# Latent attention by pairs of heads: rope halves stacked, one value product for two heads, softmax scaling on ScalarE, VectorE in another order

## The chip, the core and the metric

One core of a Trainium2 chip. The time is device microseconds from the start to the end of one execution; the kernel before takes 1957.33 us, the median of 3 runs (1956.78 to 1957.35).

## The reference, cut to what matters

Four transformer layers follow one another over 256 context and 256 latent tokens of width 1024: latent attention (layer 0), gated linear attention, a short convolution, and an mLSTM; each has a four times wider squared-relu MLP. Shift, scale and gate rows of every layer come from a vector by a large matrix product. The change is in the mixer of layer 0, with 8 heads:

```python
cq = rms_norm(h_all @ w_dq, g_q)                     # 512 x 384
q = (cq @ w_uq).reshape(B, T, 8, 128 + 64)           # 128 columns without rope, 64 with it
ckv = h_all @ w_dkv
kv = (rms_norm(ckv[..., :256], g_kv) @ w_ukv).reshape(B, T, 8, 128 + 128)   # keys, values
q_rope, k_rope = ...                                 # rotated for the 256 latent tokens only
s = einsum(q_nope, k_nope) + einsum(q_rope, k_rope)  # k_rope is one for all heads
p = softmax(s * 192 ** -0.5);  o = einsum(p, v)
y = o.reshape(T, 1024) @ w_o
```

Latent queries see all 512 tokens, context queries the 256 context tokens.

## The kernel before, in words

**Numbers.** A float32 weight block is split into a high and a low part (type fp32r); `mm3` (L721 to L732) makes one product of three single-pass matmuls: high by high (L725), high by low (L731), low by high (L732). `mm` (L734) on plain float32 operands is one instruction that shows as two records in the trace.

**The weight ring.** SP loads the blocks into 4 raw buffers. `take` (L391) is called by every engine once for each block, in its own program: it first splits the block four ahead, so that ring buffer n mod 5 is filled again (`split`: ScalarE writes the high part, L1608 to L1613, after waiting until the block five before was used; VectorE the low one, L2249 to L2257, after ScalarE), and then calls `pump`, which adds `rate` to a credit and performs one background unit for each whole credit. A unit on VectorE is four operations of 512 columns that add to the modulation sums of two token types (L2262 to L2287; the first of a sum has two plain multiplications, L2278). Its operands come by POOL's DMA into three buffers. A `close` of kind finish follows some units later: TensorE transposes the sum into a PSUM bank (L787), VectorE reduces it (L2348). For the gate rows (parts 2 and 5) it is ScalarE's high copy, VectorE's low part and a product with ones. Slots near the ends of a stage are `quiet`, and `ensure` does what is still missing when a stage needs it.

**PSUM.** Eight banks in one queue: `take` pops the front one, `give` puts it at the end at once, and TensorE waits before its first write until whoever read the bank eight takes ago has emptied it.

**The attention.** Blocks: per head one of 192 query columns by 384 rows (3 x 192 = 576 columns wide in the buffer) and one of 256 by 256 (512 wide). TensorE's order for h = 0 to 8 (L1147 to L1157): `queries(h+1)` (the 128 plain columns and the 64 rope columns, 9 matmuls of 512 columns each, L1053), `keys(h+1)` (keys 6 of 512, values 24 of 128 columns, rope rotation 64 x 64 by 256, L1071), `weights(h-1)` (12 transposes of the probabilities, L1109), `scores(h)` (L1093: plain and rope product for two latent tiles of 512 keys and two context tiles of 256), `values(h-1)` (L1121: twelve records of 256 columns into bank o). Below, pass h is what TensorE does from the end of `scores(h-1)` to the end of `scores(h)`. ScalarE copies queries and keys, takes exp with the row sum (L1872) and copies o (high part, L1886). VectorE copies the values (L2633) and the rope queries (L2625), rotates them (L2612 to L2616), finds the row maxima (L2643), negates and scales them (L2645), takes reciprocals (L2649), scales the probabilities (L2651), copies half of the transposed ones (L2660), and last in the pass subtracts for o's low part (L2665), which empties the bank of o. Its `take` calls stand at the head of `queries` and `keys`. `proj_last` then multiplies by w_o in 4 takes of 24 matmuls each, followed by `ensure` for the gate rows.

## Time and profile before

| | |
|---|---|
| median of 3 runs | 1957.33 us |
| profiled execution, its own time | 1955.74 us |
| its span, first to last instruction | 1953.9 us |
| mean granted TensorE clock | 0.998 |
| DMA | 315.16 MB, mean 161 GB/s |

Busy time is a union of an engine's instructions; durations are in ns or us as marked, starts in us from the start of the span. A matmul's duration includes its way through the array, so successive starts give its pace. The numbers of records include one weight load (PEld) for each matmul.

### The profile page before, as it was taken

What the parts mean: (1) busy time and instruction counts of PE and PEld (TensorE: products, weight loads), DVE (VectorE), ACT (ScalarE), POOL (GpSimd) and SP (SyncE); (2) the same over time, 40 slices, a digit from 0 to 9 for tenths busy, and PEclk for the clock granted to TensorE, in tenths of its full rate; (3) what the DMA queues carried; (4) which work ended last, traced back from release to release, by engine and by line L of the source; (5) the groups of instructions that cost most, each with busy time, mean ns of one, the idle gap of its engine ahead of it and who ended that gap; (6) DMA issues with size and microseconds to landing.
All of it is one profiled execution on the core that took longest, in us unless ns stands there. A gap on an engine that the chain in (4) does not pass through costs nothing.

```text
span 1953.9 us, 27442 instructions
## 1 busy us (share of the span) xinstructions
PE 1908.0 (98%) x10261; PEld 1601.7 (82%) x10261; DVE 1404.8 (72%) x2250; ACT 899.7 (46%) x1541; POOL 251.4 (13%) x334
## 2 busy tenths in 40 slices
PE   8999999999999999999999999999999999889998
PEld 3877788888888786889988888888888878878997
DVE  5889777888866665487997676667755567667765
ACT  3433355333343553575554224634233454656554
POOL 2101010111110110411101001001110021331000
PEclk9999999999999999999999999999999999999999
DMA  8434235665663451368875422645555245337763
GB/s 310 138 97 141 70 104 183 208 191 173 195 191 103 142 184 33 98 228 265 267 243 168 145 98 75 199 158 184 162 172 162 78 152 173 98 97 228 230 194 116
DMA packets 191891, 315.16 MB, mean 161 GB/s; under 512 B 14693, under 2 KB 114368, under 8 KB 191760
## 3 DMA queue, kind: packets, MB, share of 16 engines
q1 hardware_dynamic: 162512, 210.09, 33.4%
q0 software_dynamic: 29248, 103.33, 17.4%
q8 instruction: 82, 1.34, 0.3%
q14 instruction: 49, 0.40, 0.1%
HBM read 312.32 MB, written 1.05 MB: 160 GB/s over the span
## 4 chain that ended last, share of the span: by engine, by line
PE 81%; DVE 9%; issue 4%; ACT 3%; DMA 2%; POOL 1%; SPq 0%; DVEq 0%; POOLq 0%; ACTq 0%
PE bank L725 24%; PE bank L732 22%; PE bank L731 22%; PE bank L735 8%; DVE w L2256 3%; DVE acc L2281 2%; PE bank L730 2%; PE bank L728 2%; ACT junk L1645 1%; PE bank L787 1%; POOL st L3281 1%; PE bank L811 1%; DMA raw<-in_mlp_w 1%; DVE X L2400 1%; ACT w L1613 1%
## 5 line engine op out<-in xcount | busy, mean ns | idle before, releaser
L1613 ACT ACTIVATE w<-raw 128x1024 fp32r<-128x1024 f32 (+4 forms) x390 | 399.1, 1031 | 542.0 <-PE bank L732 469.3
L2256 DVE TENSOR_TENSOR w<-raw,w 128x1024 fp32r<-128x1024 f32 (+3 forms) x372 | 438.8, 1188 | 220.6 <-ACT w L1613 220.2
L725 PE MATMUL bank<-HH,w 128*128 128x256 f32 (+1 forms) x1552 | 505.7, 326 | 3.4 <-DVE HH L2383 2.0
L731 PE MATMUL bank<-HL,w 128*128 128x512 f32 (+1 forms) x1232 | 412.3, 335 | 0.0
L732 PE MATMUL bank<-HH,w 128*128 128x512 f32 (+1 forms) x1232 | 412.1, 335 | 0.0
L2281 DVE SCALAR_TENSOR_TENSOR acc<-ada,sc,acc 128x512 f32<-128x512 f32 x518 | 362.2, 745 | 2.3
L725 PEld LDWEIGHTS bank<-HH,w 128*128 128x128 f32 x1552 | 290.6, 187 | 30.4 <-issue 4.4
L725 PE MATMUL bank<-w,UH 128*128 128x512 f32 x768 | 300.7, 392 | 0.6 <-DVE UL L2558 0.6
L732 PE MATMUL bank<-w,UL 128*128 128x512 f32 x768 | 299.2, 390 | 0.0
L731 PE MATMUL bank<-w,UH 128*128 128x512 f32 x768 | 298.9, 389 | 0.0
L732 PEld LDWEIGHTS bank<-HH,w 128*128 128x128 f32 x1232 | 230.3, 187 | 26.0
L731 PEld LDWEIGHTS bank<-HL,w 128*128 128x128 f32 x1232 | 230.4, 187 | 25.6 <-issue 0.2
L732 PEld LDWEIGHTS bank<-w,UL 128*128 128x128 f32 x768 | 144.2, 188 | 30.3
L725 PEld LDWEIGHTS bank<-w,UH 128*128 128x128 f32 x768 | 144.2, 188 | 30.1 <-ACT w L1613 1.0
L731 PEld LDWEIGHTS bank<-w,UH 128*128 128x128 f32 x768 | 144.3, 188 | 29.1
L3218 POOL DMA_DIRECT2D ada<-in_mod_w x96 | 69.5, 725 | 525.1 <-DVE acc L2281 525.1
L725 PE MATMUL bank<-w,HH 128*128 128x512 f32 (+2 forms) x336 | 128.6, 383 | 1.9 <-issue 1.9
L732 PE MATMUL bank<-w,HL 128*128 128x512 f32 (+2 forms) x336 | 126.7, 377 | 0.0
L731 PE MATMUL bank<-w,HH 128*128 128x512 f32 (+2 forms) x336 | 126.5, 376 | 0.0
L2558 DVE TENSOR_TENSOR UL<-tp,UH 128x256 fp32r<-128x256 f32 (+1 forms) x128 | 69.7, 556 | 76.0 <-ACT UH L1804 75.6
L3218 POOL DMA_DIRECT2D ada<-in_ada_w x80 | 58.0, 726 | 353.4 <-DVE acc L2281 353.4
L1796 ACT ACTIVATE ta<-bank 128x256 f32<-128x256 f32 (+1 forms) x128 | 62.4, 488 | 79.1 <-PE bank L732 76.0
(365 smaller groups left out, 2605.2 us busy)
## 6 DMA issues: line engine op xcount, KB each, us to landing
raw<-in_mlp_w SPq DMA_DIRECT2D x256, 512.0 KB, 4.4
ada<-in_mod_w POOLq DMA_DIRECT2D x96, 512.0 KB, 4.7
ada<-in_ada_w POOLq DMA_DIRECT2D x80, 512.0 KB, 4.7
raw<-in_ml_w_qkvo SPq DMA_DIRECT2D x28, 512.0 KB, 3.8
raw<-in_conv_w_in SPq DMA_DIRECT2D x24, 512.0 KB, 4.1
raw<-in_ada_w SPq DMA_DIRECT2D x12, 512.0 KB, 6.2
raw<-in_mla_w_o SPq DMA_DIRECT2D x8, 512.0 KB, 4.0
raw<-in_gla_w_v SPq DMA_DIRECT2D x8, 512.0 KB, 3.8
```

The source lines that it names most:

```text
L725: pe.matmul(o, sh, mh, start=start, stop=False, skip_group_check=True)
L728: pe.matmul(o, sl, mh, start=False, stop=False, skip_group_check=True)
L730: return pe.matmul(o, sh, ml, start=False, stop=stop, skip_group_check=True)
L731: pe.matmul(o, sh, ml, start=False, stop=False, skip_group_check=True)
L732: return pe.matmul(o, sl, mh, start=False, stop=stop, skip_group_check=True)
L735: return pe.matmul(o, st, mv, start=start, stop=stop, skip_group_check=True)
L1613: act.activation(k.halves(n)[0], k.raw[(NDIRECT + n) % NRAW][:, 0:m], ACT.Copy).then_inc(*k.w_hi.up("w hi", n))
L1796: act.activation(t1[:, 0:N], b[:, 0:N], ACT.Relu).then_inc(*b.emptied())
L2256: dve.tensor_tensor(low, k.raw[(NDIRECT + n) % NRAW][:, 0:m], high.bitcast(F32), ALU.subtract).then_inc(*k.w_lo.up("w lo", n))
L2281: i = dve.scalar_tensor_tensor(out=o, in0=k.ada[m % NADA][:, q, :], scalar=cc, in1=o, op0=ALU.mult, op1=ALU.add)
L2558: dve.tensor_tensor(UL[:, n, 0:N], t2[:, 0:N], UH[:, n, 0:N].bitcast(F32), ALU.subtract).then_inc(*k.u_lo.up("u lo", li, q, n))
L3218: pool.dma_start(k.ada[m % NADA][:], src).then_inc(*k.ada_in[m % NADA].up("ada in", m, by=16))
```

## The change

- Heads go in pairs p. Weights: a block `first` of 3 x 256 columns (head 2p with its rope columns, and the rope columns of head 2p+1), `second` of 3 x 128, and `both` with keys and values of both heads (2 x 512). 12 blocks instead of 16; the stage has 28 slots instead of 32, and its rate goes from 1.2 to 1.6; slot 11 is quiet too.
- The 64 rope rows of the two heads are stacked into 128 rows: one query product, one rotation (the matrix is 128 x 128). For the scores the rope rows of a head are split: `QR` holds high and low part one above the other, `KRH` the high keys twice, `KRL` the low keys twice, and two fp32r matmuls take the place of the plain float32 one.
- One value product of 256 columns for two heads (24 matmuls a pair). It stands in the even passes, after `keys(h+1)`, and is the last reader of block `both`.
- The two context tiles of the scores share a bank, and so do those of the transposed probabilities: 3 banks instead of 4.
- ScalarE: multiplies the queries by 192 ** -0.5 as it copies them, copies the values, the rope queries and the high rope halves, the whole transposed context part, and scales the probabilities (`scaled`) behind its copy of o.
- VectorE: maxima negated as they are found, three instead of four, two reciprocals instead of four; subtracts for the low rope halves (`rope_low`). Its order: one `take` at the head of passes 1 to 6, then the low part of o of two heads before; a second `take` in odd passes, ahead of the maxima.
- In `whole` (L376 to L384) a chunk counts as whole where its step "leading" is still to be done; before, where "low" was. POOL's memsets of the rope rows go, its three constant loads are 128 rows high.

The core of the diff:

```diff
         a, e = self.at, self.at + LENGTH[li][which]
-        first, last = {(0, 0): (range(a + 5, a + 11), 4), (1, 0): (range(a + 1, a + 5), 16),
+        first, last = {(0, 0): (range(a + 5, a + 12), 4), (1, 0): (range(a + 1, a + 5), 16),
                        (3, 0): (range(a + 1, a + 9), 18)}.get((li, which), (range(a + 1, a + 5), 4))
         self.quiet = set(first) | set(range(e + 1 - last, e + 1))
...
     def whole(self):
 
-        whole = [end[1:4] for _, _, end in self.closing if end[0] == "low"]
+        whole = [end[1:4] for _, _, end in self.closing if end[0] == "leading"]
         closing, self.closing = self.closing, []
         for n, key, end in closing:
...
 
-    for name, h in [("q", 0), ("q", 1), ("kv", 0), ("kv", 1)] + [(name, h) for h in range(2, 8) for name in ("q", "kv")]:
-        c = 192 if name == "q" else 256
-        yield wide(A["mla_w_u" + name][0][:, h * c:(h + 1) * c].rearrange("(k p) n -> p k n", p=128))
+    WQ = A["mla_w_uq"][0].rearrange("(k p) n -> p k n", p=128)
+    WKV = A["mla_w_ukv"][0].rearrange("(k p) n -> p k n", p=128)
+    for p in range(4):
+        c = p * 384
+        first = (WQ[:, :, c:c + 192], WQ[:, :, c + 320:c + 384])
+        both = WKV[:, :, p * 512:(p + 1) * 512]
+        second = WQ[:, :, c + 192:c + 320]
+        for block in (first, both, second) if p else (first, second, both):
+            yield wide(block)
     yield from tokw(A["mla_w_o"][0], 0, D, 0, D)
...
+            self.KRH, self.KRL = sb("KRH", [128, 512], F32R, s1), sb("KRL", [128, 512], F32R, s1)
+            self.QR = [sb(f"QR{i}", [128, 512], F32R, s1) for i in range(2)]
-        self.VV = [self.Y[:, o:o + 512].rearrange("p (t n) -> p t n", t=4) for o in (2816, 3328, 0)]
+        self.VV = [self.Y[:, o:o + 1024].rearrange("p (t n) -> p t n", t=4) for o in (2816, 0)]
+        self.PTl = self.Y[:, 1024:2048].rearrange("p (k n) -> p k n", k=4)
+        self.PTc = self.Y[:, 2048:2560].rearrange("p (k n) -> p k n", k=2)
...
-LENGTH = [(32, 64), (33, 64), (32, 64), (37, 64)]
-RATE = [(1.2, 1.05), (0.65, 0.45), (0.4, 0.8), (0.8, 0.35)]
+LENGTH = [(28, 64), (33, 64), (32, 64), (37, 64)]
+RATE = [(1.6, 1.05), (0.65, 0.45), (0.4, 0.8), (0.8, 0.35)]
...
+        def rope_queries(p):
+            b = ps.take("rope", p)
+            w.wait_ge(*b.before())
+            w.wait_ge(*ps.of("qr", p).is_empty())
+            mm(b[:, 0:256], k.rot, k.qx[:, 256:512]).then_inc(*b.filled())
+            ps.give(b)
+
+        def from_queries(key, wh, wl, c):
+            b = ps.take(*key)
...
+            return b
+
+        def first_queries(p):
+
             n = walk.take()
             wh, wl = block_ready(n)
+            from_queries(("qr", p), wh, wl, 128)
+            block_used_with(n, from_queries(("qn", 2 * p), wh, wl, 0))
+
+        def second_queries(p):
+            n = walk.take()
+            wh, wl = block_ready(n)
+            block_used_with(n, from_queries(("qn", 2 * p + 1), wh, wl, 0))
+
+        both = {}
+
+        def keys(h):
+            if h % 2 == 0:
+                both[h // 2] = walk.take()
+            wh, wl = block_ready(both[h // 2])
+            c = h % 2 * 256
             b = ps.take("kn", h)
...
+        def pair_values(p):
+            n = both[p]
+            wv = [x.rearrange("p q (h n) -> p q h n", h=2)[:, :, :, 128:256] for x in block_ready(n)]
+            bs = [ps.take("v", p, j) for j in range(2)]
             for t in range(4):
+                b = bs[t // 2]
+                w.wait_ge(*b.before())
+                o = b[:, t % 2 * 256:t % 2 * 256 + 256].rearrange("p (h n) -> p h n", h=2)
                 for q in range(2):
-                    p = mm3(b[:, t * 128:t * 128 + 128],
-                            (k.CKH[:, q, t * 128:t * 128 + 128], k.CKL[:, q, t * 128:t * 128 + 128]),
-                            (wh[:, q, 128:256], wl[:, q, 128:256]), q == 0, q == 1)
-            p.then_inc(*b.filled())
-            block_used_with(n, b)
-            ps.give(b)
-            rope(h, k.qr[h % 2][0:64, :], ps.of("qr", h).is_empty())
+                    m = mm3(o, (k.CKH[:, q, t * 128:t * 128 + 128], k.CKL[:, q, t * 128:t * 128 + 128]),
+                            (wv[0][:, q], wv[1][:, q]), q == 0, q == 1)
+                if t % 2:
+                    m.then_inc(*b.filled())
+            block_used_with(n, bs[1])
+            ps.give(*bs)
 
...
+            def score(o, c, nk):
+                mm(o, k.qn[i][:, c:c + 128], k.kn[i][:, 0:nk], True, False)
+                mm(o, k.QR[i][:, c:c + 128], k.KRH[:, 0:nk], False, False)
+                return mm(o, k.QR[i][:, c:c + 128], k.KRL[:, 0:nk], False, True)
+
+            for t in range(2):
+                b = ps.take("s", h, 1, t)
+                w.wait_ge(*b.before())
+                score(b[:, :], 256 + t * 128, 512).then_inc(*b.filled())
+                ps.give(b)
+            b = ps.take("s", h, 0)
+            w.wait_ge(*b.before())
+            for t in range(2):
+                p = score(b[:, t * 256:t * 256 + 256], t * 128, 256)
+            p.then_inc(*b.filled())
+            ps.give(b)
...
-        queries(0)
+        first_queries(0)
         for f in (5, 3, 4):
             turned(f)
-        rope("k", k.krT[0:64, :], ps.of("cqT", 5).is_empty())
-        queries(1)
+        rope_keys()
+        second_queries(0)
+        rope_queries(0)
         keys(0)
         for h in range(9):
-            if 0 < h < 7:
-                queries(h + 1)
-            if h < 7:
+            if h % 2 and h < 7:
+                first_queries((h + 1) // 2)
                 keys(h + 1)
+                rope_queries((h + 1) // 2)
+            elif h % 2 == 0 and h < 8:
+                if h:
+                    second_queries(h // 2)
+                keys(h + 1)
+                pair_values(h // 2)
             if h > 0:
                 weights(h - 1)
...
+        def rope_queries(p):
+            b = ps.of("qr", p)
+            w.wait_ge(*b.full())
+            if p:
+                w.wait_ge(*at("rope lo", p - 1, 1))
+            act.activation(k.qx[:], b[:, :], ACT.Copy, scale=SC).then_inc(*b.emptied())
...
-                walk.take()
             b = ps.of("qn", h)
...
+        def rope_high(p, i):
+            r = i * 64
+            w.wait_ge(*at("roped", p))
+            if p:
+                w.wait_ge(*ps.of("s", 2 * p - 2 + i, 0).full())
+            act.activation(k.QR[i][r:r + 64, :], k.qx[r:r + 64, :], ACT.Copy).then_inc(*k.rope_hi.up("rope hi", p, i))
+
+        def pair_values(p):
+            for j in range(2):
+                b = ps.of("v", p, j)
+                w.wait_ge(*b.full())
+                if p >= 2:
+                    w.wait_ge(*ps.of("o", 2 * p - 3).full())
+                act.activation(k.VV[p % 2][:, 2 * j:2 * j + 2, :], b[:, :].rearrange("p (t n) -> p t n", t=2),
+                               ACT.Copy).then_inc(*b.emptied())
+
...
+        def scaled(h):
+            i = h % 2
+            rec = k.st_p[:, i, 2, :]
+            for half, P, j in ((1, k.Pl, 0), (0, k.Pc, 2)):
+                w.wait_ge(*at("p recip", h, half))
+                w.wait_ge(*ps.of("s", h, 0).is_empty())
                 for t in range(2):
-                    b = ps.of("s", h, half, t)
-                    st = k.st_p[:, i, half * 2 + t, :]
-                    w.wait_ge(*at("score max", h, half, t))
-                    if h >= 2:
...
+        rope_queries(0)
         queries(0)
         for f in (3, 4):
             turned(f)
         walk.take()
+        walk.take()
         queries(1)
+        keys_rope_high()
+        walk.take()
         keys(0)
+        rope_high(0, 0)
+        rope_high(0, 1)
         for h in range(9):
-            if 0 < h < 7:
+            if h % 2 and h < 7:
+                walk.take()
+                rope_queries((h + 1) // 2)
                 queries(h + 1)
-            if h < 7:
                 keys(h + 1)
+            elif h % 2 == 0 and h < 8:
+                if h:
+                    walk.take()
+                    queries(h + 1)
+                keys(h + 1)
+                pair_values(h // 2)
             if h > 0:
                 weights(h - 1)
+            if h % 2 and h < 7:
+                rope_high((h + 1) // 2, 0)
+                walk.take()
             if h < 8:
                 scores(h)
             if h > 0:
                 values(h - 1)
+            if h < 8:
+                scaled(h)
+            if h % 2 and h < 7:
+                rope_high((h + 1) // 2, 1)
...
+            w.wait_ge(*k.roped.last())
+            dve.tensor_tensor(k.ropet[0:n, :], b[0:n, 0:256], k.cs[0:n, 1, :], ALU.mult).then_inc(*b.emptied())
...
+        def rope_low(p, i):
+            r = i * 64
+            w.wait_ge(*at("rope hi", p, i))
+            dve.tensor_tensor(k.QR[i][64 - r:128 - r, :], k.qx[r:r + 64, :], k.QR[i][r:r + 64, :].bitcast(F32),
+                              ALU.subtract).then_inc(*k.rope_lo.up("rope lo", p, i))
...
+            b = ps.of("s", h, 0)
+            w.wait_ge(*b.full())
+            dve.reduce_max(mx[:, 2:4], b[:, :].rearrange("p (t n) -> p t n", t=2), AX.X,
+                           negate=True).then_inc(*k.score_max.up("score max", h, 0))
+
+        def reciprocals(h):
+            i = h % 2
+            tot, rec = k.st_p[:, i, 1, :], k.st_p[:, i, 2, :]
+            for t in range(2):
+                w.wait_ge(*ps.of("s", h, 1, t).is_empty())
+            dve.reciprocal(rec[:, 0:2], tot[:, 0:2]).then_inc(*k.p_recip.up("p recip", h, 1))
+            w.wait_ge(*ps.of("s", h, 0).is_empty())
+            dve.reciprocal(rec[:, 2:4], tot[:, 2:4]).then_inc(*k.p_recip.up("p recip", h, 0))
...
         for h in range(9):
+            if h % 2 == 0 and 0 < h < 8:
+                rope_low(h // 2, 1)
             if 0 < h < 7:
-                queries(h + 1)
-            if h < 7:
-                keys(h + 1)
+                walk.take()
+            if h > 1:
+                values(h - 2)
+            if h % 2 and h < 7:
+                rope((h + 1) // 2, k.qx, 128)
             if h > 0:
                 weights(h - 1)
+            if h % 2 and h < 7:
+                rope_low((h + 1) // 2, 0)
+                walk.take()
             if h < 8:
                 scores(h)
-            if h > 0:
-                values(h - 1)
+                reciprocals(h)
+        values(7)
```

## Rows read from the trace of the kernel before

**Rows 1.** The page: span, and busy us, share and instructions of each engine.
```profile
span 1953.9 us, 27442 instructions
...
PE 1908.0 (98%) x10261; PEld 1601.7 (82%) x10261; DVE 1404.8 (72%) x2250; ACT 899.7 (46%) x1541; POOL 251.4 (13%) x334
```

**Rows 2.** Stretch in the attention: us, busy PE, PEld, DVE, ACT, POOL, clock, DMA.
```profile
134.00:152.00 18.00, 18.00 (x94) 13.62 (x93) 16.82 (x38) 5.79 (x13) 2.17 (x3) 1.00 0.41 125
```

**Rows 3.** Timeline of TensorE (start, duration, instruction, count): scores 0, output 7.
```profile
98.25 0.59 PE L735 MATMUL bank<-krT,qr 128*128 128x256 f32 x2
...
227.54 1.03 PE L735 MATMUL bank<-PTc,Y 128*128 128x256 f32 x4
```

**Rows 4.** The same view: runs of single-pass matmuls of 128, 512 and 256 columns.
```profile
104.81 0.27 PE L732 MATMUL bank<-w,CKL 128*128 128x128 f32 x1
...
107.16 0.28 PE L732 MATMUL bank<-w,CKL 128*128 128x128 f32 x1
...
119.09 0.58 PE L725 MATMUL bank<-CQH,w 128*128 128x512 f32 x1
119.51 0.39 PE L731 MATMUL bank<-CQL,w 128*128 128x512 f32 x1
...
123.18 0.39 PE L732 MATMUL bank<-CQH,w 128*64 128x512 f32 x1
...
799.73 0.28 PE L731 MATMUL bank<-HL,w 128*128 128x256 f32 x1
...
801.58 0.28 PE L732 MATMUL bank<-HH,w 128*128 128x256 f32 x1
```

**Rows 5.** The same view: P^T V of one head, float32 products of 256 columns.
```profile
116.69 1.89 PE L735 MATMUL bank<-PTl,Y 128*128 128x256 f32 x8
118.41 1.03 PE L735 MATMUL bank<-PTc,Y 128*128 128x256 f32 x4
```

**Rows 6.** The same view: rope rotation, transposes, and a pass later the transposes again.
```profile
127.96 0.64 PE L735 MATMUL bank<-qr,Y 64*64 64x256 f32 x2
128.53 1.09 PE L1117 MATMUL bank<-ident,Pl 128*128 128x128 f32 x8
...
146.91 1.09 PE L1117 MATMUL bank<-ident,Pl 128*128 128x128 f32 x8
```

**Rows 7.** Groups of VectorE in the attention: count, busy us, mean ns, idle before.
```profile
L2643 DVE TENSOR_REDUCE st_p<-bank 128x1 f32<-128x512 f32 x16 | 10.9, 684 | 4.4 <-PE bank L735 4.4
...
L2651 DVE TENSOR_SCALAR Pl<-Pl,st_p 128x512 f32<-128x512 f32 x16 | 7.8, 487 | 0.6
...
L2256 DVE TENSOR_TENSOR w<-raw,w 128x1024 fp32r<-128x1024 f32 x4 | 4.9, 1216 | 0.7 <-ACT w L1613 0.7
```

**Rows 8.** Groups of ScalarE in the attention, same columns.
```profile
L1872 ACT ACTIVATE Pl<-bank,st_p 128x512 f32<-128x512 f32 x16 | 11.0, 687 | 35.9 <-DVE st_p L2645 35.8
...
L1886 ACT ACTIVATE HH<-bank 128x512 fp32r<-128x512 f32 x8 | 4.8, 598 | 12.9 <-PE bank L735 12.9
...
L1613 ACT ACTIVATE w<-raw 128x1024 fp32r<-128x1024 f32 x4 | 4.2, 1058 | 3.1 <-PE bank L732 3.1
```

**Rows 9.** Timeline of VectorE: a background step, the first operation of a finish, a sum's opening.
```profile
139.80 2.73 DVE L2281 SCALAR_TENSOR_TENSOR acc<-ada,sc,acc 128x512 f32<-128x512 f32 x4
142.46 0.68 DVE L2348 TENSOR_REDUCE sums<-bank 128x4 f32<-128x512 f32 x1
143.37 0.88 DVE L2278 TENSOR_SCALAR acc<-ada,sc 128x512 f32<-128x512 f32 x2
```

**Rows 10.** A stretch with the clock as its third number from the end; TensorE's rows there.
```profile
108.00:112.00 4.00, 4.00 (x16) 3.10 (x17) 3.90 (x9) 0.98 (x2) 0.72 (x1) 0.57 0.65 197
...
107.94 0.61 PE L735 MATMUL bank<-qr,Y 64*64 64x256 f32 x2 [0.51 <-DVE qr L2625]
108.49 1.94 PE L1117 MATMUL bank<-ident,Pl 128*128 128x128 f32 x8
```

**Rows 11.** Waits in the attention: total us, times, longest us.
```profile
PE bank L735 <- DVE sums L2348: 2.2, 1, 2.2
```

254 lines of the change are left out of this document (120 added, 134 removed).

## The prediction

> **What bounds the kernel now.** I read the page first, then the table of stretches, then TensorE's own rows. TensorE is busy for 98% of the span, VectorE for 72%, ScalarE for 46% [rows 1]. In the attention the table tells more: of a stretch of 18 us TensorE fills 18.00 at full clock, VectorE 16.82, ScalarE 5.79 [rows 2]. So TensorE bounds this part, VectorE stands close behind it, and ScalarE has room. The first head's scores end at 98.68 us (98.25 and two records of 0.215), the last head's P^T V at 228.40 (227.54 and four) [rows 3].
>
> **TensorE's part, step by step.** Starts of successive records give the pace: single-pass matmuls take (123.18-119.51)/16 = 0.229 us at 512 columns, (107.16-104.81)/21 = 0.112 at 128 and (801.58-799.73)/16 = 0.116 at 256 [rows 4]. Twice the columns cost almost nothing below 256. A plain float32 product is two records: at 256 columns they pace 0.215 (eight in 118.41-116.69), so 0.43 us, and twice that, 0.86, at 512 [rows 5].
> - Rope part of the queries: one matrix of 128 rows for two heads, so 9 of 36 products a pair go: 4 x 9 x 0.229 = 8.2 us.
> - Values: 48 products of 128 columns a pair become 24 of 256: 4 x (48 x 0.112 - 24 x 0.116) = 10.3 us.
> - Scores: the rope product becomes two single passes. Per head 2 x (0.86-0.46) + 2 x (0.43-0.23) = 1.2, by 8 = 9.7 us. No single pass follows a float32 product within one sum so far. The nearest switch: four P^T V records from 118.41 end their pace at 119.27, the next kind starts at 119.09, 0.18 early, and its follower comes 0.42 later, 0.19 late [rows 4, 5]. Both together are 0, the lateness alone is 0.2; I take 0, and up to 6.4 us for 32 switches as the bound.
> - Rope rotation: one instead of two a pair; from its start to the next 0.57 pass, 0.14 more than two records pace [rows 6]: 4 x 0.57 = 2.3 us. It may gain up to 0.6 more if the 128-row form has no such gap.
> Sum: 30.5, say 31 us less TensorE work. Alone it would give 1926. TensorE is the fullest engine by the page and by the stretch [rows 1, 2]. The Trainium skill, "Perfetto Trace Analysis", section Identifying Performance Opportunities, says that kernels generally improve by improving the most-contended engine; by this rule the sum would be 1926, a gain of 31, which is rival 1 below. No row of before contradicts it. What speaks against it here is the order of the waits, next.
>
> **VectorE and ScalarE.** VectorE loses, per head, the scaling of probabilities (0.49 and less for each of four), the negations, two reciprocals, the value copy, the query copy, half the rope and the context's P^T copy, and gains a 64-row subtraction; its four maxima become three of 0.68 [rows 7]. With 0.6 to 0.7 for an operation of 512 columns and two thirds of it for 256 that is some 4.5 us a head less. ScalarE gains four scalings, 2.0 us (nearest its 512-column copy 0.60), the value copy 0.6 and half-width copies [rows 8]; twice its 5.8 us a pass still leaves room. So no engine is over-full. The background modulation work doesn't shrink: a step costs 2.7 us (2.1 when it opens a sum), a finish 0.9 [rows 9], and at rate 1.6 it comes in lumps. Following the credit, VectorE's takes 12 to 20 hold: step-finish-step-finish; step; step, step, finish; step, finish; two steps; step, finish, step, finish; one; step, step, finish; step, finish.
>
> **The order is what I expect to decide.** Three facts of the diff meet. (a) The block with keys and values of both heads is last read by the pair's values, after the second query block is taken. A take splits the block four ahead into a ring of five, so in each even pass (heads 2, 4, 6) ScalarE's split waits until TensorE has finished the values. VectorE's low half waits for that, and its background steps stand behind. (b) VectorE now empties the output bank of head h-2 after the take, where it did so at the end of the pass. (c) Eight banks go round strictly: counting takes, the bank of o(h-2) is wanted again by a transposition of the same pass (the third in pass 2 and 6, the second in pass 4).
> Even pass 2, from the end T of head 1's scores: TensorE does P^T V 2.6 (12 records at 0.216 [rows 5]), a modulation column 0.36, queries 2.06, keys 1.38, values 2.8: T+9.2. ScalarE splits 768 columns 0.85: 10.1. VectorE: low 0.9, two steps 5.4, a finish 0.9, output 0.6: 17.9. TensorE resumes: last transposes 0.45, scores 3.95: T+22.3, where its own work is 14.5. Pass 4 has two modulation columns (9.6), 1024 columns to split (1.06 and 1.2: 11.8), two steps and two finishes (7.4), output 0.6, and two rows of transposes to go: T+24.7 against 14.8. Pass 6: 9.2, 1.06, 1.2, one step and finish 3.7, 0.6, 0.45, 3.95: T+20.2 against 14.5. Before, a pass is 18.38 (128.53 to 146.91) [rows 6].
> Odd passes: the last maximum ends at T+0.75, the exps of the context at 2.0 (two, somewhat under the 0.69 of 512 columns [rows 8]), the output copy 0.6 behind P^T V at 3.2, the scaling at 5.2; then ScalarE's split 1.06 and VectorE's low 1.2 end at 7.5 (6.5 in pass 1, which has no output). Pass 1: two steps and two finishes end at 13.7; the scores want the bank that the second finish empties at 13.5: 13.5 + 3.95 = 17.4. Pass 3: 7.5, step 2.7, finish 0.9, output 0.6 is 11.7; one transposition set 0.45 and scores 3.95: 16.1. Pass 5: opening step 2.1 and output 0.6 to 10.2, rope 1.1, P^T 0.6, rope low 0.6 to 12.5, split and low to 14.2, two steps and the sum of a finish to 20.3; the context scores (1.3) want that bank: 21.6. Pass 7 has no query work to hide the scaling: 5.2, two sets of transposes left, scores: 9.4. Tail: P^T V 2.6, scaling to 5.2, transposes and copies to 6.2, P^T V 2.6: 8.8.
> Sum from the first scores' end: 17.4 + 22.3 + 16.1 + 24.7 + 21.6 + 20.2 + 9.4 + 8.8 = 140.5, against 228.40-98.68 = 129.7: 10.8 more. Ahead of it queries 2.06, values 2.6, scores 1.2 and rope bubbles go: 7.2 less. The first rope chain (rotation 1.1, half-width copies 0.6 each on ScalarE, four subtractions 0.6 each and three splits on VectorE, all behind takes 9 and 10) ends at about 86.8 where TensorE asks at 98.68-7.2-3.95 = 87.5; it costs nothing, up to 3 if a load is late. Net +3.6.
> **Output projection.** Take 21 now holds two steps and the low halves, and take 22 the gate product that needs them: VectorE is done at 8.9 us after the attention, TensorE asks at 5.5 (24 x 0.229): about +3.
> **Clock.** A break of 0.51 us ahead of 107.94 was followed by a stretch at the lower of the two clock levels, 1.2 GHz: eight transposes took 1.94 instead of 1.09. Over 108 to 112 us the mean granted clock is 0.57, a loss of 4 x 0.43 = 1.7 us [rows 6, 10]. The longer break on the modulation sums, 2.2 us [rows 11], had no such fall. So a break costs 0 to 1.75. Mine last 6 to 10 us in four places: I take 1.75 for each, +7 (bounds 0 and 12).
> **Taken as nothing.** SP's loads (the first block of a pair comes in two pieces, 16 issues for 16 before), POOL's 128-row constants and the memsets that go: TensorE's work on the four blocks ahead hides them; a late one would show as a wait of the split for a DMA. The changed test for a whole chunk and slots moved by one in later layers: at most a wait like the 2.2 us [rows 11] here or there. Together -2 to +3.
> **Sum**: +3.6 + 3 + 7 = +13.6. The profiled execution, 1955.7 with 1953.9 of span, would become 1969.3; against the median of 1957.3 the forecast is 1971.
>
> **The rivals.**
> 1. *The order doesn't bind*: VectorE, relieved of 36 us, keeps ahead and TensorE runs dense: 1957.3 - 31 = 1926. For it: in the kernel before only 2.2 us of TensorE's time in the attention went to a bank that a finish held [rows 11]. Against: that row shows the very kind of wait, at 1.2 steps a take and with the output emptied early. Chance 0.17.
> 2. *It binds in part*: only the three even passes and one odd stall, half as long, without the clock: -31 + 18 = 1944. Chance 0.16. Ends between 1936 and 1955.
> 3. *Slower still*: every one of the breaks, the short ones too, costs clock (7 x 1.75 = 12 instead of 7), each float32 switch its 0.2 (6.4) and the gate products wait on both chunks (3 more): 1971 + 14 = 1985 and above. Chance 0.08.
> The diff does what it says; I give nothing to the opposite.
> The forecast is itself the slower side; it turns at the point where new waits, clock included, exceed 31 us, and it counts some 45.
>
> **How the numbers follow.** Forecast 0.59, its own range 1959 to 1984; rivals 0.17, 0.16, 0.08. A change under 0.2% (3.9 us) is about what this measurement can't tell from none. Slower: 0.59 less a thin low edge of 0.02, plus 0.08 = 0.65; same 0.05, from the edges of forecast and rival 2; faster 0.30. The range leaves out half of rival 1 and nearly all of rival 3: 1930 to 1984.
>
> **What would show it.** Right: TensorE idle of 5 to 10 us before the second or third transposition in passes 2, 4 and 6, released by VectorE's output subtraction; ScalarE's split waiting 2 us and more for the values' matmuls; passes alternating about 17 and 22 us; the lower clock after the breaks. Single steps: values 24 x 0.116 a pair, rope product 0.46 and 0.23, scores 3.95 a head. Wrong: passes of 14 us with TensorE at 18.00 of 18.00, or VectorE idle while TensorE works.

## The result, and the profile after

The changed kernel takes 1990.04 us (median of 4 runs, 1987.36 to 1990.86) against 1957.05 of the kernel before, measured beside it (1956.25 to 1957.35): ratio 1.0167, 95% interval 1.0154 to 1.0181. It is slower, as forecast, but by 33 us where 14 were forecast, and the time lies above the range. The profiled execution took 1989.45 us with a span of 1987.7; before, 1955.74 and 1953.9.

The page of the changed kernel, beside [rows 1]:

```profile
span 1987.7 us, 27077 instructions
...
PE 1895.1 (95%) x10121; PEld 1595.5 (80%) x10121; DVE 1375.6 (69%) x2132; ACT 927.2 (47%) x1590; POOL 249.8 (13%) x331
```

Only ScalarE is a little fuller than before (47% against 46%). TensorE's busy time fell by 12.9 us only, because part of what is left ran at half clock. Below, "clock loss" is TensorE's busy time times (1 - granted clock), added up in stretches of 1 us. From 60 to 300 us it is 1.7 us before and 16.1 now, and TensorE's idle time there is 4.8 and 47.9. Over the whole span the clock loss is 3.4 and 19.3, so the work without it fell by 28.8 us. Stretches of the attention, with the columns of [rows 2]:

```profile
120.00:140.00 20.00, 11.99 (x62) 9.49 (x61) 9.42 (x15) 7.12 (x13) 1.45 (x2) 0.75 0.26 79
160.00:180.00 20.00, 10.01 (x63) 8.93 (x62) 14.04 (x26) 8.98 (x20) 2.89 (x4) 0.86 0.40 122
220.00:240.00 20.00, 12.71 (x57) 9.11 (x56) 9.45 (x17) 9.68 (x21) 0.72 (x1) 0.83 0.17 52
```

Where TensorE filled 18.00 of 18.00 us before, it now fills 50 to 64% in these three stretches (73% over passes 1 to 8, 97% before), while VectorE fills 47 to 70% and ScalarE 36 to 48%: no engine is short of time, they wait for each other in turn. TensorE's waits from 60 to 300 us (total us, times, longest):

```profile
PE bank L1170 <- DVE HL L2786: 16.3, 4, 8.0
PE bank L1161 <- DVE HL L2786: 10.0, 1, 10.0
PE bank L751 <- DVE sums L2474: 9.7, 2, 6.7
PE bank L1058 <- DVE Y L2710: 3.6, 1, 3.6
PE bank L1161 <- ACT Pl L1977: 2.8, 2, 1.4
PE bank L751 <- DVE accl L2450: 2.6, 1, 2.6
```

Before, the only entry above 1.2 us there was the 2.2 us of [rows 11]. Two of the new names are those that the prediction gave: the low part of o (HL) in front of the transposes, and the modulation sums in front of the scores. The fourth, a scaling of cq ahead of the attention, it did not have.

TensorE's timeline, the last score record of heads 0, 1, 2 and 7, and the last P^T V:

```profile
97.14 0.28 PE L751 MATMUL bank<-KRL,QR 128*128 128x256 f32 x1
...
117.37 0.28 PE L751 MATMUL bank<-KRL,QR 128*128 128x256 f32 x1
...
142.33 0.28 PE L751 MATMUL bank<-KRL,QR 128*128 128x256 f32 x1
...
243.79 0.28 PE L751 MATMUL bank<-KRL,QR 128*128 128x256 f32 x1
...
250.58 2.83 PE L751 MATMUL bank<-Y 128*128 128x256 f32 x12 [0.78 <-ACT Y L1987]
```

Start plus duration is the end of a head's scores. The differences of the eight ends are the passes 1 to 7: 20.2, 25.0, 16.4, 27.9, 23.3, 24.2 and 9.7 us, and pass 8 has 9.2 to the end of P^T V (253.2: twelve records at a pace of 0.215).

Pass 2 shows how a break is made. VectorE, and TensorE below it:

```profile
128.02 0.96 DVE L2382 TENSOR_TENSOR w<-raw,w 128x768 fp32r<-128x768 f32 x1 [3.75 <-ACT w L1673]
128.90 5.38 DVE L2407 SCALAR_TENSOR_TENSOR acc<-ada,sc,acc 128x512 f32<-128x512 f32 x8
134.20 0.68 DVE L2474 TENSOR_REDUCE sums<-bank 128x4 f32<-128x512 f32 x1
134.92 0.16 DVE L2427 TENSOR_TENSOR mod<-sums,bgc 128x4 f32<-128x4 f32 x1
135.11 0.69 DVE L2786 TENSOR_TENSOR HL<-bank,HH 128x512 fp32r<-128x512 f32 x1
```

```profile
126.82 1.03 PE L1161 MATMUL bank<-ident,Pl 128*128 128x128 f32 x8
135.86 1.11 PE L1170 MATMUL bank<-ident,Pc 128*128 128x128 f32 x4 [8.01 <-DVE HL L2786]
136.77 1.91 PE L751 MATMUL bank<-kn,qn 128*128 128x512 f32 x2
```

VectorE idles 3.75 us for ScalarE's split, does its low half, two background units (eight operations, 5.4 us) and a finish, and only then the subtraction that frees o's bank. The two float32 records behind the break take 1.91 us instead of 1.02: the clock is at its lower level.

The loss by stretches, each the difference of the two traces at the same work: first scores 1.3 us earlier (97.4 against 98.7 [rows 3]); end of the attention 24.8 later (253.2 against 228.4); first transposes behind the output projection 29.5 later (297.9 against 268.3); the same until 666 us; then +30.6 at 871, +30.2 at 1068, +34.6 at 1239, and 33.8 at the end.

### The profile page after: what moved, and what is told of

Its sections match the earlier page's. It is cut to its first block, busy times and chain, and to the rows that moved or that the text cites. A ratio compares the mean times of both kernels' runs of the same rounds, so it can differ in the third digit from the quotient of the medians.

```text
span 1987.7 us, 27077 instructions
## 1 busy us (share of the span) xinstructions
PE 1895.1 (95%) x10121; PEld 1595.5 (80%) x10121; DVE 1375.6 (69%) x2132; ACT 927.2 (47%) x1590; POOL 249.8 (13%) x331
## 4 chain that ended last, share of the span: by engine, by line
PE 78%; DVE 11%; issue 5%; ACT 4%; POOL 1%; DMA 1%; SPq 0%; DVEq 0%; POOLq 0%; ACTq 0%
PE bank L741 23%; PE bank L748 21%; PE bank L747 21%; PE bank L751 8%; DVE acc L2407 3%; DVE w L2382 3%; PE bank L746 2%; PE bank L744 2%; ACT junk L1705 1%; ACT w L1673 1%; PE bank L803 1%; POOL st L3413 1%; PE bank L827 1%; DVE X L2526 1%; DMA raw<-in_ada_w 1%
## 5 line engine op out<-in xcount | busy, mean ns | idle before, releaser
L1673 ACT ACTIVATE w<-raw 128x1024 fp32r<-128x1024 f32 (+2 forms) x386 | 398.3, 1040 | 552.8 <-PE bank L748 466.7
```

Source lines behind the costliest of these rows:

```text
L1673: act.activation(k.halves(n)[0], k.raw[(NDIRECT + n) % NRAW][:, 0:m], ACT.Copy).then_inc(*k.w_hi.up("w hi", n))
```

## The experiments

All times are medians of at least four runs; the kernel before took 1955.6 to 1956.9 in the groups. A ratio's 95% interval is about 0.0015 to either side, 3 us, so smaller differences between two versions are read from their traces or not at all. "The slots' work" below is what a slot's take brings: a split and background units (one chunk's quarter each, 2.7 us of VectorE). Later edits are shown against the one before.

**1. The low part of o ahead of the take.**

```diff
+            if h > 1:
+                values(h - 2)
             if 0 < h < 7:
                 walk.take()
-            if h > 1:
-                values(h - 2)
```

> Edit: VectorE makes the low part of o of the head before ahead of the slot's take (split and background unit) instead of behind it; nothing else. Theory (banks are held by several late readers, the o bank only the last of them): the modulation bank, whose sums VectorE also closes late, binds next; 3 to 8 us less than the changed kernel, and breaks of the transposes of Pl and Pc still there, with the modulation sums named as releaser. Rival (the o bank's order alone makes the breaks): the breaks of 8.0, 10.0 and 5.9 us go and with them their clock, 25 to 34 us less, about the time of the kernel before.

Measured: 1984.67, 5.4 less, and not the 25 to 34 of the rival. It is the theory's size and its next wait: the low part is named for 1.3 us, and the sums take over.

```profile
PE bank L751 <- DVE sums L2474: 24.4, 6, 6.8
PE bank L1170 <- DVE sums L2474: 5.7, 2, 3.7
...
PE bank L1161 <- DVE HL L2786: 1.3, 1, 1.3
```

26 us of waits left one name and 20 came back under another. A name in the list of waits says who was last, not what the time would be without it.

**2. One unit a slot in slots 1 to 4.**

```diff
-        self.credit += self.rate
+        self.credit += 1.0 if self.at <= 4 else self.rate
```

> Edit: one background unit a slot in slots 1 to 4, as before the change (4 units instead of 6), 1.6 a slot behind them. Theory: VectorE scales cq in time again, the first scores end 5 to 6 us earlier, and the two units that move into the attention passes give 0 to 3 of it back: 3 to 6 us less than the changed kernel. Rival (the start ahead of the attention is hidden by the passes' own breaks, which wait for VectorE anyway): 0 to 1 us less.

Measured: 2000.40, 10.4 more: both expectations missed. The first half held: queries start at 74.3 instead of 78.3 and the first scores end 3.8 us earlier. The two units came back in the passes (end of the attention only 1.1 earlier), and the rest was lost far away: against the kernel before the later stages stand at +27.3, +33.2, +38.3, +38.7, +41.8, +41.4, +44.8, and the end at +45.9. Run 5 looks into that.

**3. Keys and values ahead of the second queries** (TensorE, and ScalarE's copies in that order).

```diff
-                if h:
-                    second_queries(h // 2)
                 keys(h + 1)
                 pair_values(h // 2)
+                if h:
+                    second_queries(h // 2)
```

> Edit: in even passes TensorE takes the keys of the next head and the pair's values ahead of the second queries, and ScalarE copies in that order, so that the block of keys and values is free before the slot's split asks for it. Theory: the splits of passes 2, 4 and 6 come 1.5 to 3.3 us earlier, VectorE's take is shorter by that, and the breaks behind it too: 3 to 6 us less than the changed kernel. Rival (the split waits, but VectorE is late for its own units): 0 to 1 us less.

Measured: 1983.47, 6.6 less: with all else as it is, fact (a) of the prediction costs that much, at the place where it was put.

**4. The three together.**

> The three edits of this group together. Theory: the gains add, since they are at different places, and breaks above 5 us lose their half-clock stretches as well: 15 to 22 us less than the changed kernel, so still slower than the kernel before by 11 to 18 us. Rival (one chain through VectorE, so the edits overlap): 6 to 12 us less. Rival (the o bank alone): 30 us or more less, faster than the kernel before.

Measured: 1976.68, 13.4 less, between the theory's 15 to 22 and the first rival's 6 to 12. The attention ended at 230.2, 23 us earlier, twice the sum of the three alone (6.1, 4.3 and 1.1 by their traces): each had uncovered the next wait, and together they take both. But behind the output projection, where it stood at +5.0 against the kernel before, it lost 17.4 more up to the end, as run 2 did (18.7).

**5. The fraction that is carried on.** The rate is added up in slots, and what is left of a unit at the end of the attention goes into all later layers.

```diff
         self.rate = RATE[li][which]
+        if (li, which) == (0, 1):
+            self.credit = 0.0
```

> Edit: the changed kernel, and the fraction of a background unit that 17 slots of 1.6 leave over (27.2, so 0.2) is set to nothing at the start of layer 0's second half, as 17 slots of 1.0 left it before; the slots of all later units are then those of the kernel before. Theory (the 4.3 us that the changed kernel loses between 840 and 1205 us come from those moved slots): 4 us less than the changed kernel (3 to 5), and its break of 2.1 us near 1068 us back at 0.6. Rival (they come from the cores' clock or from chance): within 1 us of it.

Measured: 1992.75, 2.7 more, which neither expectation had. My count was wrong: the kernel before has 32 slots with 22 that add 1.2, which leaves 0.4 and not 0. So this was no return to its order. Repeated with `self.credit = 0.39999999999999925`, the kernel before's own value:

> Edit: the changed kernel, with the fraction of a unit that is carried into layer 0's second half set to 0.4, which is what 22 slots of 1.2 leave in the kernel before (with 27.2 it is 0.2, and the run with nothing was based on a wrong count). Theory: the later layers then meet the kernel before's order, so the marks from 666 us on stay 29.5 us behind and the time is 4 us less than the changed kernel, 1985 to 1987. Rival (later losses come from the time of arrival, not from the order): within 1 us of the changed kernel or above it.

Measured: 1988.79, only 1.3 less; the ratio (1.0161, 1.0146 to 1.0176) does not tell it from the changed kernel. But the trace agrees with the theory up to 1600 us: this kernel stands 27.9 us behind at 296 us, and 27.9, 27.9, 27.6, 27.6, 27.6 at the next five stages, where the changed kernel goes from 29.5 to 34.6. Then it loses 3.6 up to 1793 and 1.0 more behind, in the last layer, so that the stages behind the output projection cost 4.3 in all, as in the changed kernel. Over all runs, what these stages cost against the kernel before, by the fraction they start with: 2.8 to 5.0 us at 0.2, 9.2 to 13.9 at nothing, 17.4 and 18.7 at 0.8. At 0.4 it is 4.3 to 5.7 with the changed test in `whole`, and 2.5 and less with the old one (runs 10 and 12). Slots that move by one there are not free, and the fraction is not the only thing that counts.

**6. The three edits with the fraction at nothing, and closing ahead of the unit.** The edit of the second:

```diff
-        self.unit(unit)
+        if self.at > 24:
+            self.unit(unit)
         for c in self.closing:
             c[0] -= 1
         self.flush(0)
+        if self.at <= 24:
+            self.unit(unit)
```

> The three edits of the first group together, and the fraction set to nothing as in the run beside it. The three together ended the attention 23 us earlier than the changed kernel but lost 16 us against the kernel before in the later layers, with a fraction of 0.8. Theory (the fraction is what costs there): 14 to 16 us less than with the three alone, 1961 to 1964. Rival (the units left over for the output projection cost, whatever the fraction): 3 us less at the most.

> As the run before it in this group, and up to slot 24 VectorE closes modulation sums (one reduction and one addition, 0.9 us) ahead of the unit that makes them due, not behind it (2.7 us), so that their bank comes free by that much earlier. Theory (with o's bank out of the way the modulation banks bind): the breaks named by the sums, 20.6 us in six, shrink by 2.7 us each where a unit stood in front: 6 to 12 us less than the run before it. Rival (VectorE is short of time in the passes, so what is closed earlier is paid by later maxima): 0 to 2 us less.

Measured: 1974.34 and 1969.08. The first rests on the same wrong count and fell (2.3 less than the three alone, not 14 to 16); its rival held. Its stages behind the output projection still cost 13.9 us instead of 17.4. The second gave 5.3 of the 6 to 12: the attention ends 6.5 us earlier, so the time for which a modulation bank is held did bind.

**7. Units placed by hand.** First with `STEPS` of one or two a slot in slots 12 to 20 and extra places only behind the copy of P^T (passes 2, 4, 6, 7 and 8) and at the head of passes 7 and 8; then with one at the head of each pass, where VectorE idles.

> As the run before it in this group, and the background units go to places by hand: one in each of slots 1 to 4, two or three in each of passes 1 to 6, each at a place of its own (behind the copy of the turned probabilities in passes 2, 4 and 6), and two in each of passes 7 and 8, which had none; so none is left for a lump ahead of the output projection's end. Theory (lumps of two units, 5.5 us of VectorE, make the breaks; its total of work fits under TensorE's): breaks in the passes under 6 us in all, no stretch at half clock, 10 to 18 us less than the run before it, and below the kernel before (under 1950). Rival (VectorE's total binds): within 4 us of the run before it.

> As the hand-placed run, with: one unit of VectorE's at the head of each pass right behind the low part of o, where VectorE idles 3 us for the split, and one behind it in passes 1 to 6 (two in pass 6); none between the copy of the turned probabilities and the maxima; the low part of the second rope half behind that copy; one unit between the two scalings of cq and ckv; and the fraction of a unit that is carried into the later layers as the kernel before has it (22 slots of 1.2: 0.4; the expectation of the run with the fraction at nothing said 17 slots of 1.0, which is wrong). Theory: passes 1 to 6 take 14 to 16 us each, so 10 to 14 us less up to the output projection than the hand-placed run, and the 5 us that it lost against the kernel before behind 633 us stay away as well: 1944 to 1952. Rival (VectorE and ScalarE hand over too often for a pass of 15 us): 1955 to 1962.

Measured: 1964.35, then 1936.89. The first fell short of its 10 to 18 (4.7, which the intervals hardly tell from none): even passes were down to 15.4 and 14.6, passes 3 and 5 stayed at 23.4 and 23.6, because in the even pass two units and two finishes stood ahead of the copy of P^T, for which TensorE's next product then waited 5.0 us. The second took passes 2 to 6 to 15.2, 14.2, 14.6, 14.2 and 14.6 us, and was faster than its own range. The edit of the second against the changed kernel, besides those above (`pump(n)` adds n to the credit; a slot takes its number from STEPS; the other engines call it at the same places of their order):

```diff
+STEPS = {1: 1, 2: 1, 3: 1, 4: 1, 12: 1, 14: 1, 15: 1, 17: 1, 18: 1, 20: 2, 21: 1, 22: 1, 23: 1, 24: 1}
+HEAD = {1: 1, 2: 1, 3: 1, 4: 1, 5: 1, 6: 1, 7: 1, 8: 1}
+MID = {7: 1, 8: 2}
+PRE = 1
...
         for f in range(3):
             turned(f)
+        walk.pump(PRE)
         mean_square(1, 256)
...
-            if h % 2 == 0 and 0 < h < 8:
-                rope_low(h // 2, 1)
             if h > 1:
                 values(h - 2)
+            walk.pump(HEAD.get(h, 0))
             if 0 < h < 7:
                 walk.take()
...
             if h > 0:
                 weights(h - 1)
+            if h % 2 == 0 and 0 < h < 8:
+                rope_low(h // 2, 1)
+            walk.pump(MID.get(h, 0))
```

**8. Light units.** Is it the work between two hand-overs, or the hand-overs themselves? This kernel leaves out the middle accumulations of slots 12 to 20 and keeps every order, bank and split.

```diff
+                elif 12 <= walk.at <= 20 and not (q == 1 and ty == types[-1]):
+                    continue
                 else:
                     w.wait_ge(*added[ty])
                     i = dve.scalar_tensor_tensor(
```

> Edit: the changed kernel, and the background units of slots 12 to 20 leave out those accumulations of the modulation sums that are neither first nor last of their unit (three of four of 0.69 us each in most units; these sums, and so the output, are left incomplete); order, banks and splits are kept. Theory (VectorE's background work, held in lumps between the reads of the banks, makes the breaks): breaks of the passes from 36 us to under 10, no stretch at half clock, 28 to 36 us less than the changed kernel, 1954 to 1962. Rival (the order of hands between ScalarE and VectorE around o and the splits makes them, whatever the work between): 8 us less at the most.

Measured: 1962.92, 27.1 less, a little outside the expected range; the rival's 8 fell. In the passes TensorE's idle time went from 41.5 us to 21.7 and its clock loss from 12.7 to 5.9, so the breaks fell by half and not to under 10:

```profile
PE bank L1170 <- DVE HL L2788: 8.1, 2, 4.2
PE bank L1161 <- DVE HL L2788: 6.0, 1, 6.0
PE bank L751 <- DVE sums L2476: 4.0, 2, 3.0
```

So 27 of the 33 us hang on the time that VectorE's units take where they stand, though VectorE is busy for only 119.6 of the 200 us from 60 to 260.

**9. Filled breaks.**

```diff
+                for _ in range({(1, 1): 50, (3, 0): 60, (5, 1): 36}.get((h, t), 0)):
+                    pe.transpose(b[:, 0:128], k.ident[:], k.ident[:])
```

> Edit: the changed kernel, and TensorE turns the identity 50, 60 and 36 times into the bank that it owns, ahead of the last transposes before the breaks of 8.0, 10.0 and 5.9 us, so that most of each break is filled with work that nobody reads. Theory (a break of that length costs 2.1 to 2.7 us more behind it, because the clock is at its lower level from then on for 7 to 10 us): breaks down to about 2 to 3 us, the half-clock stretches near 140, 185 and 236 us gone, 4 to 7 us less than the changed kernel. Rival (the clock falls whatever fills the break, or VectorE's chain hides it anyway): within 1 us of the changed kernel.

Measured: 1985.91, 4.1 less with 146 transposes more (1982.8 to 1988.3 against 1987.4 to 1990.9; the two intervals of the ratio overlap a little). The break of 8.0 us became 5.6 of unread work and 2.5 of break. TensorE's stretches (busy, then granted clock); the changed kernel first, the filled one second:

```profile
130.00:140.00 10.00, 4.14 (x9) 0.50 0.52 157
...
180.00:190.00 10.00, 10.00 (x37) 0.77 0.11 42
220.00:230.00 10.00, 4.09 (x19) 0.78 0.34 105
```

```profile
130.00:140.00 10.00, 7.45 (x37) 0.83 0.45 139
...
180.00:190.00 10.00, 10.00 (x42) 0.90 0.01 2
220.00:230.00 10.00, 8.02 (x49) 1.00 0.36 105
```

The clock stayed at full level behind the third break (2.4 us of pass 6 came back) and fell for a shorter time behind the other two (0.7 and 1.0 us). In this trace 1.3 us came back in pass 1 too, where nothing was filled: the clock varies by that much without any edit. The clock loss in passes 2, 4 and 6 together went from 8.4 to 4.3 us. So a part of each long break's price is the clock, and not the wait. The Trainium skill, "TensorE: Matmul & The Clock Gate", section Loop structure matters more than you think, says that the loop nest decides whether matmuls stay at the fast clock; by this run the trace agrees, with the 8.4 and 4.3 us above. Here unread work in the loop stood in for read work.

**10. The old test for whole sums, and fewer late units.**

```diff
-        whole = [end[1:4] for _, _, end in self.closing if end[0] == "leading"]
+        whole = [end[1:4] for _, _, end in self.closing if end[0] == "low"]
```

The second has `20: 1` in STEPS and `MID = {8: 2}`.

> As the second hand-placed run, and the test by which a gate's sum that is due at once goes through one float32 product is the kernel before's again (it asks for the low part still to be made, the changed kernel's for both parts). VectorE's order behind the attention is then that of the kernel before, instruction by instruction; with the changed test one gate of the last layer makes a low part, and TensorE waits 2.2 us for it. Theory: 3 to 4 us less than the second hand-placed run (1933 to 1934), the wait of 2.2 us near 1700 us gone. Rival (the wait moves elsewhere in that layer): within 1 us of it.

> As the run before it in this group, with one unit less in pass 6 and none between pass 7's copy of the turned probabilities and its maxima; both go to the output projection (layer 0 keeps the changed kernel's test, the later layers the old one). Theory (a unit ahead of the copy costs TensorE 2.5 us in pass 7, one ahead of the maxima 3.3 us in pass 8): passes 7 and 8 take 10.5 to 11.5 us instead of 13.3 and 12.3, 2 to 5 us less, 1929 to 1932. Rival (the projection's slots give them back at its gate): within 1 us of it or above.

Measured: 1934.58 and 1928.73. The wait of 2.2 us on a gate's low part in the last layer (in the second hand-placed run and in the one with 0.4) is gone, and 2.3 us with it, where 3 to 4 were expected. The second keeps the changed test in layer 0, where the old one would close a sum whole without waiting for a high part that ScalarE has already begun. Its passes 7 and 8 take 11.8 and 11.1 instead of 13.3 and 12.1, and it is 5.9 us faster than the run before. Two things changed at once, and of the 7.4 us between the two traces only 2.5 lie in these passes: 2.2 lie ahead of the first scores, 1.7 of that a clock loss that the run before had there, and 2.7 behind the output projection. Its ratio to the kernel before is 0.986 (95%: 0.9846 to 0.9875). The largest waits of TensorE from 60 to 300 us (two more, of 0.7 and 0.4, end the list):

```profile
PE bank L1173 <- ACT Pl L1992: 2.7, 2, 1.9
PE bank L763 <- DVE Y L2800: 2.6, 2, 2.3
```

VectorE in its pass 5, units one at a time and o's bank freed first:

```profile
150.63 0.69 DVE L2805 TENSOR_TENSOR HL<-bank,HH 128x512 fp32r<-128x512 f32 x1 [0.84 <-ACT HH L2007]
151.23 2.73 DVE L2425 SCALAR_TENSOR_TENSOR acc<-ada,sc,acc 128x512 f32<-128x512 f32 x4
...
156.01 2.74 DVE L2425 SCALAR_TENSOR_TENSOR acc<-ada,sc,acc 128x512 f32<-128x512 f32 x4
```

The later stages stand at -29.3, -29.3, -29.4, -29.5, -29.5, -29.5, -29.5 against the kernel before: nothing moves behind the attention any more. The Trainium skill, "Perfetto Trace Analysis", section Optimization Strategy, says that a repeated bubble on the engine that should be full can mean too little PSUM for the next tile. Here the eight banks are the same in the changed kernel and in this one: their readers' order and the lumps were at fault, not their number.

**11. The rate alone, in both kernels.**

In the kernel before:

```diff
-RATE = [(1.2, 1.05), (0.65, 0.45), (0.4, 0.8), (0.8, 0.35)]
+RATE = [(1.6, 1.05), (0.65, 0.45), (0.4, 0.8), (0.8, 0.35)]
```

> Edit: the kernel before (not the changed one), with 1.6 background units a slot instead of 1.2 in layer 0's first half, so 6 instead of 4 in slots 1 to 4 and lumps of two in the heads' slots. Theory (the lump ahead of the attention costs 5 us of start by itself; the kernel before has its breaks filled by 31 us more of TensorE's work and its o bank is freed by ScalarE at once, so lumps cost it little): 2 to 8 us more than the kernel before, 1959 to 1965. Rival (lumps are what makes the changed kernel slow, in any order of work): 20 us more or above, 1977 or more.

Measured: 1980.25, 24.7 more, ratio 1.0124 (1.0107 to 1.0141). The theory fell and the rival held: this one number costs the kernel before three quarters of what the change cost. It is not the rate's share of the 33 us, though. The first half of layer 0 has 28 units in all, and with 22 slots at 1.6 all of them stand ahead of the attention's end, against 25 in the kernel before and 24 in the changed kernel; so its passes have lumps and more work. (The theory had one premise wrong besides: in the kernel before too o's bank is emptied by VectorE, at the end of the pass.) Its trace shows the same row ahead of the attention, with the first scores 6.2 us later, and breaks in the passes with clock behind them (clock loss in the passes 8.3 us instead of 1.7):

```profile
PE bank L735 <- DVE qr L2625: 5.3, 2, 3.0
PE bank L735 <- DVE sums L2348: 4.4, 2, 3.3
PE bank L1042 <- DVE Y L2585: 3.6, 1, 3.6
```

Taking the rate back in the changed kernel is no cure, since it has 28 slots in that half instead of 32:

> Edit: the changed kernel, with 1.2 background units a slot instead of 1.6: 4 in slots 1 to 4, 11 in the passes instead of 14 or 15, and what is left (3 or 4 units and their closings) in one lump ahead of the last columns of the output projection; its fraction is 0.4. Theory: 4 us less ahead of the attention, 3 units less at about 2.7 us of VectorE in the passes (6 to 9 us less there), 4 to 8 us more at the output projection: 5 to 9 us less than the changed kernel, 1981 to 1985. Rival (the projection waits for the whole lump, 10 to 13 us): within 2 us of it.

Measured: 1995.21, 5.2 more than the changed kernel, so both expectations missed. The attention ends 14.9 us earlier, more than expected, but what is left over stands in one lump in the output projection, which takes 20.8 us more (65.4 from the attention's end to the next transposes, 44.6 in the changed kernel):

```profile
PE bank L741 <- DVE Y L2581: 6.7, 1, 6.7
PE bank L751 <- DVE accl L2450: 5.1, 1, 5.1
PE bank L751 <- DVE acc L2407: 4.3, 1, 4.3
```

**12. The two facts of order, without lumps.** The edit of run 1 is undone in the fastest version (`values(h - 2)` again behind the take), and beside it that of run 3.

> As the fastest version so far (hand-placed units, 1928.7 us), with the low part of o behind the pass's first unit and its take again, where the changed kernel has it. Theory (the order around o binds only where lumps stand in front of it; one unit and a split are 4 us): it comes 4 to 6 us later, some transposes wait, 2 to 8 us more than the fastest version, 1931 to 1937. Rival A (the order is the fault and comes back in full): 15 us more or above, 1944 or more. Rival B (it no longer matters at all): within 1 us.

> As the fastest version so far, with the second queries ahead of the keys and the pair's values in passes 2, 4 and 6 again, as the changed kernel has them, so that the split waits for the values. Theory: the split and VectorE's work behind it come 2 to 3 us later in three passes, 2 to 6 us more than the fastest version, 1931 to 1935. Rival (with one unit ahead of the split VectorE has other work meanwhile): within 1 us.

Measured: 1943.24 (14.5 more) and 1927.16 (1.6 less, which can't be told from none). In the first the theory's 2 to 8 fell, and rival A, with 15 or more, came within 1 us. Even so this kernel is 13.2 us faster than the kernel before (ratio 0.9941, 0.9927 to 0.9955). The place of o's low part is worth more without lumps than with them (5.4 in run 1): it now binds alone, in five passes, and nothing else stands behind it.

```profile
PE bank L1182 <- DVE HL L2805: 12.8, 5, 3.1
```

The order of queries and values is worth nothing once VectorE has a unit to do while the split waits. The last kernel, with the changed kernel's own order there, is as fast as the fastest (ratio 0.9851, 0.9835 to 0.9867).

## Why the prediction was right and wrong

**Right.** The direction, the mechanism and the places: breaks of TensorE ahead of the transposes in passes 2, 4 and 6, released by o's low part, of 8.0, 10.0 and 5.9 us, where the forecast's ends less TensorE's own work give 7.8, 9.9 and 5.7; a break in pass 5 by the sums of a finish (6.7, as listed); a split of ScalarE that waits for the values (3.5 and 3.6 us in passes 2 and 6, but 0.5 in pass 4); the gate product at the projection (2.6 us, forecast 3). Single steps, on a pair of context scores:

```profile
243.24 0.59 PE L751 MATMUL bank<-kn,qn 128*128 128x256 f32 x2
243.48 0.47 PE L751 MATMUL bank<-KRH,QR 128*128 128x256 f32 x1
243.79 0.28 PE L751 MATMUL bank<-KRL,QR 128*128 128x256 f32 x1
243.91 2.75 PE L751 MATMUL bank<-Y 128*128 128x256 f32 x12
```

The float32 product gives way 0.24 after its start and the single pass comes 0.31 and 0.12 behind: 0.67 for the tile against 0.43 + 0.23 forecast, and the two shifts of the switch cancel, as the prediction took it. That TensorE's work falls by 31 is borne out by the fastest hand-placed version of run 10, whose busy time less clock loss is 31.1 us under that of the kernel before (1873.5 against 1904.6) and whose trace stands 29.5 us ahead. Rival 1 (1926) gave the change's worth; its claim that the order does not bind was wrong. The measured time lies where rival 3 was (1985 and above, chance 0.08). Its clock term of 12 held, as the next part shows; its 6.4 for the float32 switches did not.

**Wrong**, by the forecast's own terms, profiled time 1989.5 against 1969.3, 20.2 us. Two steps failed: the first term below left out what the rate does in slots 1 to 4, and the clock was mis-sized, with 16.1 us of loss from 60 to 300 us where 7 were forecast.
- *"Ahead of it ... 7.2 less"*, measured 1.3: 5.9 us. The prediction used the rate of 1.6 for takes 12 to 20 and not for slots 1 to 4, where it puts six units instead of four. VectorE then scales cq 4.9 us later than before (70.79 against 65.86), TensorE waits 3.65 for it, and a clock loss of 1.7 follows. VectorE, and TensorE's wait for it:

```profile
55.16 5.38 DVE L2407 SCALAR_TENSOR_TENSOR acc<-ada,sc,acc 128x512 f32<-128x512 f32 x8
...
65.50 4.05 DVE L2407 SCALAR_TENSOR_TENSOR acc<-ada,sc,acc 128x512 f32<-128x512 f32 x6
...
70.79 1.41 DVE L2710 TENSOR_SCALAR Y<-Y,st_cq 128x384 f32<-128x384 f32 x4 [1.16 <-POOL st_cq L3472]
```

```profile
71.36 1.03 PE L1058 MATMUL bank<-ident,Y 128*128 128x128 f32 x3 [3.65 <-DVE Y L2710]
```

  The kernel before with 1.6 has the same wait, and its first scores end 6.2 us later. This step failed in its mechanism: a wait that the prediction did not have. The saving of 7.2 itself was right: in the fastest version of run 10 the first scores end 7.0 us earlier than before.
- *The passes with the clock*: 140.5 + 7 forecast, 155.8 measured: 8.3 us. Pass by pass the forecast was 17.4, 22.3, 16.1, 24.7, 21.6, 20.2, 9.4, 8.8, so it was short by 2.8, 2.7, 0.3, 3.2, 1.7, 4.0, 0.3, 0.4. The form was right, except that passes 5 and 6 do not alternate; what was mis-sized is the clock. Its loss by passes is 2.8, 2.2, 0, 2.7, 1.5, 3.5, 0 and 0, together 12.7, where the forecast had 7 in the four long breaks and 12 as its bound: 5.7 of the 8.3. The other 2.6 are waits and work that are each a little longer. The 1.75 came from a row where the lower level lasted one short stretch, and pass 1's two short breaks were counted at nothing:

```profile
110.00:120.00 10.00, 9.31 (x28) 6.44 (x29) 8.02 (x17) 3.51 (x10) 1.44 (x2) 0.68 0.52 163
```

- *The projection's +3*: 4.7 (29.5 less 24.8), 1.7 more. The wait was 2.6; the clock, 0.83 in 260 to 270 us, cost 1.7.
- *"Taken as nothing", -2 to +3*: 4.3. Two causes are there, and neither alone is the whole: the kernel before with a fraction of 0.2 and its own test loses 3.4 behind the output projection (run 11), the changed kernel with 0.4 and the changed test 4.3 (run 5), and with 0.4 and the old test in the later layers nothing is lost (run 10).

Together 5.9 + 8.3 + 1.7 + 4.3 = 20.2. The clock has a part in each of the first three, 1.7 + 5.7 + 1.7 = 9.1 us, and is the largest single error. Two sums of the working are off by 0.1 and 0.2 us (8 x 1.2 is 9.6; two steps and two finishes are 7.2), which changes nothing.

The forecast also told half of the cause. It explained the loss by the order of hand-overs, facts (a) and (b), and took the rate as a circumstance. The rate alone costs the kernel before 24.7 us (with the reservation of run 11). In the changed kernel (a) and (b), taken away alone, give 6.6 and 5.4. With the units spread by hand the change pays even with (b) left in (run 12), and without it brings the 29 us that TensorE saves. But (b) is not small: without lumps it costs 14.5. So the lumps are what makes the kernel slow, and the order decides what they hold up.

Open: whether the kernel before would also gain from units placed by hand was not tried; its waits of TensorE from 60 to 300 us sum to 4.1 us and its clock loss there to 1.7, which leaves little to gain. The rate was not tried apart from the number of units that it brings into the passes.

## What to carry to other kernels

A constant that spreads background work belongs to the change like any instruction: follow it through every slot that it reaches, ahead of and far behind the code that is edited, and through what it leaves over. Put background work one unit at a time where its engine idles for another's hand-over anyway, and empty first the bank that comes round next. What one wait costs is known only when the next one in line is gone: the same edit was worth 5 us in one setting and 14 in another, and a second edit 7 us in one and nothing in the other.

## What the runs showed of the hardware

- The price of a break is not its length, and a short one can cost clock where a longer one does not. Five breaks of 1.95 to 3.09 us, one a pass, left the granted clock at 1.00 up to 210 us (run 12, o's low part behind). Two of 1.95 and 3.01 us within 5 us in pass 1 of the changed kernel were followed by ten us at a mean of 0.68, and the one of 10.0 us by ten at 0.77.
- Work that nobody reads is cheaper than the break that it fills: 146 more transposes, 4.1 us less by the medians (run 9).
- A switch from a float32 product to single passes within one sum costs nothing (above), and a rotation over 128 rows takes 0.43 us, start to next start, where the one over 64 rows took 0.57 [rows 6]:

```profile
103.61 0.59 PE L751 MATMUL bank<-qx,Y 128*128 128x256 f32 x2
104.04 1.03 PE L1161 MATMUL bank<-ident,Pl 128*128 128x128 f32 x8
```
